# A hybrid decoder block on one core: orders at the stage seams, and two gate pieces at another place

## The reference

```
h = rms_norm(x, g_mix) * (1.0 + sc1) + sh1
(a_q, a_k, a_v, conv_in, c_q, c_k, c_v, c_r, c_low,
 d_q, d_k, d_v, gate_logits) = split(h @ w_in)
y_a = dilated_attention_mixer(a_q, a_k, a_v, q_gain, k_gain) @ w_br_a   # windows, 3 groups x 4 heads
y_b = conformer_conv_mixer(conv_in, ...) @ w_br_b                       # depthwise conv, width 31
y_c = gla_mixer(c_q, c_k, c_v, c_r, c_low, ...) @ w_br_c                # gated linear attention
y_d = stick_breaking_mixer(d_q, d_k, d_v) @ w_br_d
gates = sigmoid(gate_logits).reshape(B, S, 4, D)
merged = gates[0]*y_a + gates[1]*y_b + gates[2]*y_c + gates[3]*y_d
x = x + gt1 * (merged @ w_out)
h = rms_norm(x, g_mlp) * (1.0 + sc2) + sh2
x = x + gt2 * (square(relu(h @ w_up)) @ w_down)
```

## Time and profile before

| | us |
|---|---|
| median of 3 runs | 1978.63 |
| lowest, highest | 1974.88, 1979.43 |
| the profiled execution | 1980.79 |
| its span | 1979.1 |
| TensorE busy | 1909.6 (96%) |
| VectorE busy | 1261.1 (64%) |
| ScalarE busy | 851.0 (43%) |
| GpSimd busy | 271.8 (14%) |
| mean granted clock of TensorE, of full speed | 0.985 |

### The profile page before, as it was taken

How to read it: one execution, slowest core, us unless ns; L and a number is a source line. 1 busy time by engine, 2 the same in 40 slices (tenths; PEclk the granted TensorE clock), 3 DMA queues, 4 the chain that set the end, 5 groups by cost and what they waited for, 6 DMA issues and landing times. The chain is left out here.

```text
span 1979.1 us, 24189 instructions
## 1 busy us (share of the span) xinstructions
PE 1909.6 (96%) x9128; PEld 1534.2 (78%) x9128; DVE 1261.1 (64%) x1576; ACT 851.0 (43%) x1350; POOL 271.8 (14%) x176
## 2 busy tenths in 40 slices
PE   5999989999999999999999999999999999999999
PEld 4887868888766677877788778788788887888887
DVE  7699951331356476638557388567766675688855
ACT  6311242331466542166664354334445444444443
POOL 0122214542221144112100000000000000000000
PEclk8999999999999999999998999999999999999999
DMA  9375432322321251344122667401354445963343
GB/s 300 122 219 161 154 115 83 123 96 75 128 59 44 67 175 53 114 168 153 57 72 65 218 229 229 164 17 54 98 163 158 140 165 204 316 203 107 96 118 101
DMA packets 221069, 266.24 MB, mean 135 GB/s; under 512 B 12266, under 2 KB 149610, under 8 KB 220954
## 3 DMA queue, kind: packets, MB, share of 16 engines
q1 hardware_dynamic: 220830, 264.66, 41.6%
q10 hardware_dynamic: 124, 0.04, 0.0%
HBM read 187.46 MB, written 77.20 MB: 134 GB/s over the span
## 5 line engine op out<-in xcount | busy, mean ns | idle before, releaser
L942 PE MATMUL dn_ps<-h_hi,dn_hi 128*128 128x512 f32 (+1 forms) x848 | 345.9, 408 | 19.0 <-ACT dn_out L322 12.3
L944 PE MATMUL dn_ps<-h_hi,dn_lo 128*128 128x512 f32 (+1 forms) x848 | 334.2, 394 | 0.0
L943 PE MATMUL dn_ps<-h_lo,dn_hi 128*128 128x512 f32 (+1 forms) x848 | 334.2, 394 | 0.0
L942 PEld LDWEIGHTS dn_ps<-h_hi,dn_hi 128*128 128x128 f32 (+1 forms) x848 | 159.8, 188 | 76.6 <-issue 41.2
L305 POOL TENSOR_TENSOR dn_lo<-dn_raw,dn_hi 128x1024 fp32r<-128x1024 f32 (+1 forms) x53 | 141.3, 2666 | 537.7 <-ACT dn_hi L301 537.7
L944 PEld LDWEIGHTS dn_ps<-h_hi,dn_lo 128*128 128x128 f32 (+1 forms) x848 | 159.5, 188 | 36.8
L322 ACT ACTIVATE dn_out<-dn_ps 128x512 f32<-128x512 f32 (+1 forms) x106 | 62.6, 590 | 290.1 <-PE dn_ps L944 250.0
L943 PEld LDWEIGHTS dn_ps<-h_lo,dn_hi 128*128 128x128 f32 (+1 forms) x848 | 160.0, 189 | 33.5 <-issue 1.2
L1506 ACT ACTIVATE tl_ring_hi<-tl_cell 128x512 fp32r<-128x512 f32 x112 | 70.6, 630 | 150.2 <-PE mg_ps_y L944 133.9
L943 PE MATMUL mg_ps_y<-tl_ring_lo,tl_ring_hi 128*128 128x512 f32 x320 | 125.0, 391 | 0.0
L942 PE MATMUL mg_ps_y<-tl_ring_hi,tl_ring_hi 128*128 128x512 f32 x320 | 125.0, 391 | 0.0
(11 more groups left out here) (481 smaller groups left out, 4286.4 us busy)
## 6 DMA issues: line engine op xcount, KB each, us to landing
tl_raw_hidden<-hidden SPq DMA_DIRECT2D x112, 256.0 KB, 2.8
dn_raw<-w_in_dram SPq DMA_DIRECT2D x54, 512.0 KB, 4.3
ada<-w_ada_dram SPq DMA_DIRECT2D x48, 512.0 KB, 7.0
logits<-dn_out SPq DMA_DIRECT2D x64, 256.0 KB, 2.2
tl_unit<-w_up_dram SPq DMA_DIRECT2D x64, 256.0 KB, 3.1
hidden<-tl_hidden_sum SPq DMA_DIRECT2D x16, 1024.0 KB, 4.9
tl_cell<-w_down_dram SPq DMA_DIRECT2D x64, 256.0 KB, 4.9
proj<-dn_out SPq DMA_DIRECT2D x40, 256.0 KB, 2.3
```

Source lines behind the costliest of these rows:

```text
L942: nc.tensor.matmul(out, w_hi[:, t, :], x_hi[:, t, :], start=begin, stop=False, skip_group_check=reopened)
L943: nc.tensor.matmul(out, w_hi[:, t, :], x_lo[:, t, :], start=False, stop=False, skip_group_check=reopened)
L944: mm = nc.tensor.matmul(out, w_lo[:, t, :], x_hi[:, t, :], start=False, stop=end, skip_group_check=reopened)
```

## The change

Nine edits of order, in five stages; one of them adds a wait on GpSimd. Lines are those of before.
- **Front.** SP's load of the second raw pair (`pairs.load(sp, 1)`) moves from step 21 to step 19; the store of the convolution's output moves from step 21, ahead of tile 19's stores, to step 22, behind tile 20's. ScalarE's first three `pairs.high` move from behind tile 21 to between the two copies of tile 22.
- **Stick-breaking.** The last of the loop's pieces moves behind the last values product.
- **Gated linear attention.** SP's last `dense.move` goes ahead of the last store of `oT`. On GpSimd the last `dense.lower` now waits for `used`, all of VectorE's last multiplies; the one before it is written out on its own.
- **Window, preparation.** `copy_values(8)` goes behind the residual of the square; step 9 has one piece in place of two, step 11 two in place of one.
- **Window, unit loop.** No pieces in iterations 20 and 22; one each in iterations 24 and 25, which had none.
- **Close.** `low_tile(2)` goes between `evict(0)` and `evict(1)`; `norm(2)` and `scale_tokens(2)` go one place forward. At the start of the up-projection the unit sums and the slot lows of the next block go ahead of the join and the hidden sums, and `difference(9)` ahead of two slot lows.

```diff
@@ stage_front, SP
                 if j == 19:
                     pairs.load(sp, 0)
-                if j == 21:
-                    sp.wait_ge(cv_out, C)
-                    sp.dma_start(feature_tiles(k.mix[Y_B * P:Y_C * P, :]), acc[:, :, :]).then_inc(k.conv_stored, 16)
                     sp.wait_ge(gated, 1)
                     pairs.load(sp, 1)
                 if j - 2 >= dense.early:
...
+                if j == FIRST_TAIL - 1:
+                    sp.wait_ge(cv_out, C)
+                    sp.dma_start(feature_tiles(k.mix[Y_B * P:Y_C * P, :]), acc[:, :, :]).then_inc(k.conv_stored, 16)
@@ stage_front, ScalarE
                 dense.copy(act, j, 0)
+                if j == FIRST_TAIL - 1:
+                    act.wait_ge(cv_out, C)
+                    for q in range(Pairs.AHEAD):
+                        pairs.high(act, q)
...
-                if j == FIRST_TAIL - 2:
-                    act.wait_ge(cv_out, C)
-                    for q in range(Pairs.AHEAD):
-                        pairs.high(act, q)
@@ stage_close, ScalarE
                 if tt == 2:
                     high(0)
+                    norm(2)
                 high(tt - 1)
-                norm(tt)
+                if tt > 2:
+                    norm(tt)
@@ stage_close, VectorE
             evict(0)
+            low_tile(2)
             evict(1)
-            low_tile(2)
             low_tile(3)
...
                 if tt == 2:
                     modulate(0)
+                    scale_tokens(2)
                 modulate(tt - 1)
-                scale_tokens(tt)
+                if tt > 2:
+                    scale_tokens(tt)
...
             sum_units(PLAIN, 4)
+            difference(9)
             for p in (P5, P7):
                 low_slot("up", PLAIN, (p,))
-            difference(9)
+            dve.wait_ge(slot_lo_ready, PLACE["up", PLAIN, (P7,)] + 1)
+            for n in (1, 2, 3):
+                sum_units(PLAIN + 1, n)
             low_difference(3)
...
+                if b == PLAIN:
+                    for p in (P1, P6):
+                        low_slot("up", b + 1, (p,))
                 if b < NB:
                     combine(b, 1)
                 sum_hidden(b - 2)
-                if b + 1 < NB:
+                if PLAIN < b < NB - 1:
                     for n in (1, 2, 3):
                         sum_units(b + 1, n)
                     for p in (P1, P6):
                         low_slot("up", b + 1, (p,))
+                if b + 1 < NB:
                     sum_units(b + 1, 4)
@@ stage_window
+    PIECE_AT = [n for n in range(N) if n % 4 < 3 and n not in (20, 22)] + [N, N + 1]
+
     def pieces_before(n):
-        return min(UNIT_PIECES, 3 * (n // 4) + min(n % 4, 3))
+        return sum(1 for at in PIECE_AT if at < n)
...
         def pieces_at(t):
 
-            return 2 if 1 <= t <= 9 else 1
+            return 2 if 1 <= t <= 8 or t == 11 else 1
...
-                if n < N:
-                    dense.pieces(pe, pieces_before(n + 1) - pieces_before(n))
+                dense.pieces(pe, pieces_before(n + 1) - pieces_before(n))
...
                 norm(t)
-                if t == 1:
-                    copy_values(8)
                 if 2 <= t < 5:
                     biases(4 * (t - 2))
                 if t + 2 < len(TILES):
                     low_square(t + 2)
+                if t == 1:
+                    copy_values(8)
@@ stage_gla
                 dense.move(sp, FROM + PREPARE + LEVEL + STATE + h)
+                if h == GLA_HEADS - 1:
+                    dense.move(sp, FROM + PREPARE + LEVEL + STATE + NORM - 1)
                 sp.wait_ge(used, 3 * h + 3)
                 sp.dma_start(k.mix[(Y_C + h) * P:(Y_C + h + 1) * P, :], oT[:, h, :]).then_inc(k.linear_stored, 16)
-            dense.move(sp, FROM + PREPARE + LEVEL + STATE + NORM - 1)
...
+            dense.lower(pool, FROM + PREPARE + LEVEL + STATE + NORM - 2)
+            pool.wait_ge(used, 3 * GLA_HEADS)
             dense.lower(pool, FROM + PREPARE + LEVEL + STATE + NORM)
@@ stage_stick
-                if n < N + LAG - 1:
+                if n < N + LAG - 2:
                     dense.pieces(pe, 1)
                 if n >= LAG:
                     values(n - LAG)
-            dense.pieces(pe, 3 * HALVES - HEAD - EACH * (N + LAG - 1))
+            dense.pieces(pe, 3 * HALVES - HEAD - EACH * (N + LAG - 1) + 1)
```

## The result

| | before | after |
|---|---|---|
| median of 5 runs, us | 1978.63 (1973.24 to 1981.01) | 1944.90 (1941.41 to 1946.38) |
| ratio to before | | 0.9833, 95% interval 0.9814 to 0.9853 |
| span of the profiled execution | 1979.1 | 1943.1 |
| TensorE (PE) busy | 1909.6 | 1896.9 |
| mean granted clock | 0.985 | 0.993 |

A forecast was written before the change was run, and what follows sets the result against it. TensorE, busy 96% of the span, was taken as the bound, gaining only by fewer stops or more full clock. Idle 21.5 plus 10.5 of 14.9 clock gave 32 us: from the median 1978.6 to 1946.6, range 1940 to 1958.

The forecast's parts named there:

- The front: Conv store behind tile 20's stores: PE's wait for the output copy goes, 7.1 us idle plus 2.3 clock.
- Stick-breaking: At its end, six matmuls behind the last values product shrink PE's barrier wait from 1.7 to about 0.4: 1.35 us.
- Gated linear attention: At its end, VectorE's multiply shortens, SP's last store goes out earlier, PE's barrier idle shrinks: 1.2 us, bounds -0.6 and 2.1.
- the end of the last of them moves: At gated linear attention's closing barrier, the last finish moves from 888.0 to between 886.8 and 887.1: 1.2 us taken.
- Preparation: Window stage: the residual's wait loses 1.3 us, the scores' wait 1.6; each is followed by 1.7 of clock.
- Unit loop: Window stage: PE's wait for the transposed probabilities goes, 2.1 us idle, plus 5.1 from the low clock behind it.
- Merge to MLP: Residual of tile 2 starts earlier, 0.9 us idle and 1.7 clock; the next tile's long wait goes, 1.5.
- Up-projection: At its start, PE's wait for the slot's low part goes: 4.5 us idle, plus 2.4 of clock.
- the seven tenths on the clock: Of 14.9 us full-clock gain, 10.5 was taken, since two stops leave a rest and a fall may come elsewhere.
- The signs: Expected afterwards: PE busy 8 to 13 us less, waits of 7.1 and 4.5 under 1, transposed probabilities' row gone.
- the two barrier rows: PE's barrier waits, ending stick-breaking and gated linear attention, were to sum to under 4 us after the change.

The follow-up runs named there:

- the front alone: Kernel before with only the three front edits (conv store, second raw pair's load, three high parts on ScalarE): 1968.22 us, ratio 0.9952.

## Why the prediction was right, step by step

- **The front, 9.4 forecast, 9.1 measured (7.1 idle, 2.0 clock).** The reading of the earlier trace rows was right, and the store alone does it.
- **Stick-breaking, 1.35 forecast.** The idle went from 1.73 to 0.47, as said. In the trace after, the clock stretch behind it, which the text left out, went too, 1.4 more; that is a chance of this execution, for it was back in three other traces of the same order. And then 2.2 were lost in the next stage, by a mechanism that the text knew (two engines that slow each other) and looked for at one place only. Net 0.5, and the two go together: where the clock is kept the loss comes, and where it falls neither.
- **Gated linear attention, 1.2 forecast, 1.6 measured, for a wrong reason.** The step that failed is "the end of the last of them moves": I let GpSimd's new end set the barrier and gave the gain to the shorter multiply. With the multiply at its old 3.30 the stop is 0.3 shorter still. The barrier itself gave 1.0 (2.50 to 1.50), and the other 0.6 was not forecast: a wait for copied values behind it, 0.91 before and 0.34 after. What was late before was SP's move, issued behind the last store; GpSimd's wait was cover for a neighbour that did no harm.
- **Preparation, 2.9 idle, 1.7 + 1.7 clock; 5.6 measured.** Right in this trace; taken back, 3.9 came back in another. The low clock of 1.7 each is not sure in a run: it came behind both stops in five traces, and behind one of the two in the sixth.
- **Unit loop, 2.1 + 5.1; 7.1 measured.** Right, with the right cause. The 5.1 is itself one value of two: behind the same idle of 2.06 the traces show 0.57 over 12 us in three cases and 0.86 in one (the front alone):

```profile
1072.60:1084.60 12.00, 12.00 (x52) 11.23 (x53) 11.52 (x31) 1.02 (x1) 1.75 (x1) 0.57 0.14 40
```

```profile
1062.00:1074.00 12.00, 12.00 (x68) 10.97 (x69) 11.52 (x31) 1.24 (x2) 1.76 (x1) 0.86 0.14 40
```

  The first is of the kernel before, the second of the front alone. In three traces the clock, once low in this work, stayed low for 10 us with PE busy all the time; at full clock the same work kept it for 29. "TensorE: Matmul & The Clock Gate" of the Trainium skill, section "What's actually happening", has the low clock as the default that activity releases. The fall behind a stop agrees with it; that PE was busy for 10.20 of 10.20 us at 0.50 shows that busy time alone did not release it at once in this work, and what did is left open.
- **Merge to MLP, 2.4 + 1.7; 4.2 measured. Up-projection, 4.5 + 2.4; 7.0 measured.** Right. In the first, 1.05 of the wait is left, against 1.0 forecast; no run has this edit alone, so the part is read from the trace only, and its clock is luck: the stop of 1.9 stands in five traces, and the clock fell behind it in two, of which the kernel before is one.
- **The sum.** Its one mis-sized term is the seven tenths on the clock: 10.5 taken, 15.0 measured. The places with a forecast gave 13.9 of the 14.9 in full (2.0, 2.6, 5.0, 1.8 and 2.5), the end of stick-breaking 1.4 more, and 0.4 was lost in gated linear attention. The idle gave 21.0 against 21.5: 1.7 lost in gated linear attention, and 1.1 gained at the gates, where nothing had been forecast. In all 36.0 by the spans against 32. The median moved by 33.7 and the span by 36.0; the spread of the runs, 5 us for the changed kernel and 8 for the one before, has room for both. That 33.7 lies so near the 32 is in part luck, since no row gave the seven tenths and several of the stretches come and go from run to run.
- **The signs.** PE's busy time fell by 12.7, within the 8 to 13. The waits of 7.1, 4.5 and for the transposed probabilities are gone (the rows of the first two keep other waits, the longest 1.5 and 1.8). One sign failed: the two barrier rows sum to 3.9 + 0.5 = 4.4 and not to under 4, though the forecast's own terms, 6.6 less 2.55, left 4.05.
